# Two transformer blocks in one kernel: a weight slot's lower part moved to GpSimd, a second PSUM bank for one attention head, and an ending with four stores

## What is computed

```python
x = x + _mixer(x, mem, ...);  x = x + _conv_ffn(x, ...)
x = _rmsnorm(x, g1)
h = x
for layer in range(2):
    hn = rmsnorm(h, norm_mix[layer])
    h = h + (hybrid_attention(hn, ...) if layer == 0 else neighbourhood_attention(hn, ...))
    h = h + sq_relu_mlp(rmsnorm(h, norm_ffn[layer]), ffn_w_up[layer], ffn_w_down[layer])
out = rmsnorm(h, final_norm)      # y = x * rsqrt(mean(x*x) + EPS), times the gain
```

## Time and profile before

| | |
|---|---|
| median of 3 runs | 1160.37 us (1159.82 to 1163.45) |
| the profiled execution | 1160.56 us |
| its span, first to last instruction | 1158.7 us |
| TensorE busy | 1143.1 us, 99% |
| VectorE busy | 840.1 us, 73% |
| ScalarE busy | 628.8 us, 54% |
| GpSimd busy | 496.7 us, 43% |
| mean granted TensorE clock | 0.999 of full |

### The profile page before, as it was taken

The page is one execution under the profiler, slowest core; times in us unless marked ns, Lnnn a source line. Parts: engine busy times, 40 slices in busy tenths (PEclk is TensorE's granted clock), DMA queues, the critical chain, the costliest instruction groups (busy, mean ns, idle before and its releaser), DMA issues.

```text
span 1158.7 us, 18483 instructions
## 1 busy us (share of the span) xinstructions
PE 1143.1 (99%) x6964; PEld 1017.0 (88%) x6964; DVE 840.1 (73%) x1099; ACT 628.8 (54%) x858; POOL 496.7 (43%) x433
## 2 busy tenths in 40 slices
PE   8999999999999999999999999999999999999997
PEld 8999999889998888888897888888888888888886
DVE  5778988986675898777898767566576676656655
ACT  7554443556634665555668755444464677444443
POOL 2799997996201543233233538880010455000000
PEclk9999999999999999999999999999999999999999
DMA  9655545563447456554552286655555514565550
GB/s 300 205 179 179 192 161 192 179 203 109 143 156 238 145 182 217 181 186 169 158 161 91 79 236 229 195 191 194 181 182 182 182 38 133 198 200 190 188 181 37
DMA packets 142665, 201.08 MB, mean 174 GB/s; under 512 B 3284, under 2 KB 123092, under 8 KB 142604
## 3 DMA queue, kind: packets, MB, share of 16 engines
q1 hardware_dynamic: 141632, 196.88, 51.5%
q0 software_dynamic: 912, 3.17, 1.2%
q10 hardware_dynamic: 60, 0.20, 0.1%
HBM read 199.20 MB, written 1.05 MB: 173 GB/s over the span
## 4 chain that ended last, share of the span: by engine, by line
PE 95%; DVE 2%; ACT 1%; issue 1%; DMA 0%; POOL 0%; POOLq 0%; DVEq 0%; ACTq 0%
PE ps L2003 52%; PE ps L2046 24%; PE ps L2049 11%; PE ps L2130 3%; PE ps L2045 2%; PE ps L2192 1%; PE ps L2112 1%; PE ps L2180 1%; DMA gates<-in_vecs 0%; ACT ps L758 0%; DVE work L1302 0%; PE ps L2098 0%; PE ps L2396 0%; PE ps L2383 0%; DVE p_parts L1309 0%
## 5 line engine op out<-in xcount | busy, mean ns | idle before, releaser
L1207 DVE TENSOR_TENSOR wlo<-raw,whi 128x2048 fp32r<-128x2048 f32 (+1 forms) x162 | 376.3, 2324 | 132.7 <-ACT whi L668 132.3
L668 ACT ACTIVATE whi<-raw 128x2048 fp32r<-128x2048 f32 (+1 forms) x178 | 337.6, 1897 | 141.0 <-PE ps L2003 133.5
L2046 PE MATMUL ps<-p_parts,whi 128*128 128x512 f32 x1184 | 414.0, 398 | 0.0
L2049 PE MATMUL ps<-p_parts,wlo 128*128 128x256 f32 x1036 | 291.2, 281 | 0.0
L2046 PEld LDWEIGHTS ps<-p_parts,whi 128*128 128x128 f32 x1184 | 216.0, 188 | 41.9
L2049 PEld LDWEIGHTS ps<-p_parts,wlo 128*128 128x128 f32 x1036 | 196.1, 189 | 5.8
L2003 PE MATMUL ps<-p_parts,whi 128*128 128x256 f32 x912 | 164.8, 284 | 0.9 <-DVE p_parts L1234 0.9
L2003 PE MATMUL ps<-whi,q_hi 128*128 128x512 f32 x380 | 148.5, 391 | 0.0
L2003 PE MATMUL ps<-wlo,q_hi 128*128 128x512 f32 x380 | 148.0, 390 | 0.0
L2003 PE MATMUL ps<-whi,q_lo 128*128 128x512 f32 x380 | 148.0, 389 | 0.0
L2003 PEld LDWEIGHTS ps<-p_parts,whi 128*128 128x128 f32 x912 | 142.4, 192 | 1.2 <-issue 1.1
(11 more groups left out here) (322 smaller groups left out, 1907.8 us busy)
## 6 DMA issues: line engine op xcount, KB each, us to landing
raw<-in_w_in SPq DMA_DIRECT2D x35, 1024.0 KB, 5.0
raw<-in_w_up SPq DMA_DIRECT2D x22, 1024.0 KB, 5.1
raw<-in_up_a SPq DMA_DIRECT2D x16, 1024.0 KB, 5.4
raw<-in_down_a SPq DMA_DIRECT2D x16, 1024.0 KB, 4.9
raw<-in_up_b SPq DMA_DIRECT2D x16, 1024.0 KB, 5.5
raw<-in_down_b SPq DMA_DIRECT2D x16, 1024.0 KB, 4.9
raw<-in_od_w_qkv SPq DMA_DIRECT2D x12, 1024.0 KB, 5.1
raw<-in_w_down SPq DMA_DIRECT2D x11, 1024.0 KB, 4.9
```

Source lines behind the costliest of these rows:

```text
L668: nc.scalar.activation(whi[:, g % R, 0:n], raw[:, g % R, 0:n], ACT.Copy).then_inc(hi_ready, 1)
L1207: nc.vector.tensor_tensor(wlo[:, g % R, 0:n], raw[:, g % R, 0:n], whi[:, g % R, 0:n].bitcast(F32), ALU.subtract).then_inc(lo_ready[g % R], 1)
L2046: ins = nc.tensor.matmul(dst, whi[:, r, at], p_parts[:, :, S * k:S * k + S], start=k == 0, stop=k == KD - 1)
L2049: nc.tensor.matmul(dst[:, 0:S], wlo[:, r, at], p_hi[:, S * k:S * k + S], start=False, stop=False)
```

## The change

Three edits. In "att2" the lower part of group G_EVO is no longer one VectorE instruction in `woven_heads`, but four pieces on GpSimd at the start of its own `woven_heads`. In "att3" head 1 gets a bank of its own, bank 4. At the end, VectorE makes the mean square of row tile 0 before its third sum and no longer after it, scales a half of row tile 0 itself (`scaled_half`), and does the last two gain products later; ScalarE scales 512 in place of 1024 columns of row tile 0, ahead of the third square; the stores are four halves in place of a tile and two halves.

```diff
-    ("qk", {0: 4, 2: 4}), ("v", HIGH4), ("att3", HEADS16), ("od_out", HIGH4),
+    ("qk", {0: 4, 2: 4}), ("v", HIGH4), ("att3", {**HEADS16, 2: 15, 4: 1}), ("od_out", HIGH4),
...
 def rows_bank(name, i):
-    if name == "att2" and i == 1:
-        return 5, USES["att2"][5]
-    return 2, USES[name][2] + i - (1 if name == "att2" and i > 1 else 0)
+    second = {"att2": 5, "att3": 4}[name]
+    if i == 1:
+        return second, USES[name][second]
+    return 2, USES[name][2] + i - (1 if i > 1 else 0)
...
-            for done, n, t, part in ((fin_act, 1, 0, slice(0, D)), (fin_dve, 1, 1, slice(0, BW)), (fin_act, 2, 1, slice(BW, D))):
+            for done, n, t, part in ((fin_act, 1, 0, slice(0, BW)), (fin_dve, 1, 0, slice(BW, D)), (fin_dve, 2, 1, slice(0, BW)), (fin_act, 2, 1, slice(BW, D))):
                 sp.wait_ge(done, n)
                 sp.dma_start(out_v[:, t, part], x[:, t, part]).then_inc(out_done, 16)
-            sp.wait_ge(out_done, 16 * 3)
+            sp.wait_ge(out_done, 16 * 4)
...
                 if name == "att2":
+                    for n in range(4):
+                        lo_piece(G_EVO, n)
                     queries_keys(2)
...
             for t, m in FINAL_ORDER:
+                if (t, m) == FINAL_ORDER[2]:
+                    act.wait_ge(fin_y, 1)
+                    scaled_rows(0, slice(0, BW))
                 act.wait_ge(bank_read[4 + t + 2 * m], USES["ffn2b"][4 + t + 2 * m] + 1)
                 square_of_rows("fin2", t, m)
-                if (t, m) == FINAL_ORDER[2]:
-                    act.wait_ge(fin_y, 2)
-                    scaled_rows(0, slice(0, D))
...
                 if name == "att2":
                     maxima(name, 2)
                     maxima(name, 3)
-                    lo(G_EVO)
                     latent_keys_in((4,))
...
+            def scaled_half(t, part):
+                dve.wait_ge(norm_r, T * POW_NORMS.index("fin2") + t + 1)
+                nc.vector.tensor_scalar(x[:, t, part], xfin[:, t, part], rr[:, n + t:n + t + 1], None, ALU.mult).then_inc(fin_dve, 1)
+
             for i, (t, m) in enumerate(FINAL_ORDER):
+                if i == 2:
+                    mean_square(NORMS.index("fin2"), 0)
                 summed(i, t, m)
-                if (t, m) == FINAL_ORDER[2]:
-                    mean_square(NORMS.index("fin2"), 0)
-                times_gain(t, m)
+                if i < 2:
+                    times_gain(t, m)
+            dve.wait_ge(fin_y, 2)
+            scaled_half(0, slice(BW, D))
+            times_gain(*FINAL_ORDER[2])
             mean_square(NORMS.index("fin2"), 1)
-            dve.wait_ge(norm_r, T * POW_NORMS.index("fin2") + 2)
+            times_gain(*FINAL_ORDER[3])
             dve.wait_ge(fin_y, 4)
-            nc.vector.tensor_scalar(x[:, 1, 0:BW], xfin[:, 1, 0:BW], rr[:, n + 1:n + 2], None, ALU.mult).then_inc(fin_dve, 1)
+            scaled_half(1, slice(0, BW))
```

## The result

| | median | spread | ratio to before |
|---|---|---|---|
| before | 1160.37 us | 1159.72 to 1163.45, 10 runs | |
| with the change | 1165.38 us | 1164.51 to 1168.17, 10 runs | 1.0042, 95% 1.0033 to 1.005 |

A forecast was written before the change was run, and what follows sets the result against it. TensorE bounds the kernel, except at the second attention's start, where the chain runs 9 us through VectorE. Terms 3.3 - 0.4 - 0.3 = +2.6 us gave a median of 1163.0 us, range 1159.3 to 1165.2.

The forecast's parts named there:

- Part A: Second attention's start: slot G_EVO's lower part moves from VectorE to GpSimd; +3.3 us, between -0.3 and +4.0.
- the stall: Second attention's first query rotation: VectorE's root and three rotation operations wait for GpSimd pieces, 3.6 us, all on the path.
- The taps of the feed-forward: VectorE operations beside GpSimd pieces from 394.29 us; 4.77 us against 1.66 alone, so 1.04 us more per held operation.
- The 4.3 us: Upper bound of the delay at the first query rotation, if each held operation waits for a whole piece.
- VectorE keeps its turn: Rival at the rotations: 0.45 us wait, then 0.85 at the second rotation; 1160.7 us; chance 0.23 together with no exclusion.
- the move is all gain: Rival: latent key fills readable as early as VectorE is free, 2.9 us gained, 1157.5 us; chance 0.04.
- what the removal gives: Second attention: removing VectorE's 2.19 us instruction brings only 0.28 us through, since VectorE waits for fill 4.
- B: Last attention: head 1 in bank 4 lets head 2's transposes start 0.71 us earlier; -0.4 us in all.
- C: Kernel's end: mean square 0.7 us earlier, but last power 0.93 us in place of 0.55; -0.3 us in all.
- full clock behind the stall: After TensorE's 3.8 us idle before the unit 1 scores, the clock stays full; forecast 1162 to 1164, chance 0.58.
- The range: Whole kernel's time: 1159.3 to 1165.2 us, leaving about 0.06 below and 0.09 above.
- the clock case: Rival: TensorE's 3.8 us idle before the unit 1 scores lowers its clock, 1 to 4 us more, 1164 to 1167; chance 0.15.

The follow-up runs named there:

- the pieces put later: Whole change, but GpSimd starts its four pieces only when VectorE has done both query rotations: 1159.8 us, ratio 0.9996.
- part A alone: Kernel before with only the slot's lower part moved from VectorE to four GpSimd pieces, attention banks and ending as before: 1165.52 us, ratio 1.0047.
- the run with the filled wait: Whole change plus 16 matmuls of no use on TensorE before the scores of unit 1: 1163.11 us, ratio 1.0028.
- one piece: Whole change with one GpSimd instruction of 2048 columns in place of the four pieces: 1165.37 us, ratio 1.0042.

## Why the prediction was wrong

*Part A, the stall: right.* 3.6 us foreseen, 3.63 found in the changed kernel. Its working holds in its parts too: the root held 0.5 us (0.45 foreseen), the first rotation operation free, the next three held for a piece each, 1.29 to 1.40 us from start to start. The taps of the feed-forward were the right rows to price them by. The Trainium skill (SBUF — State Buffer, Who interferes with whom) has the mechanism: the two engines exclude each other for a whole instruction. The trace agrees. The 4.3 us that I had worked out from it took a whole piece of waiting for each held operation (by its own terms it is 0.45 + 3 x 1.25 = 4.2) and is too much, because an operation that gets ready while a piece runs waits only for its rest. The rival that VectorE keeps its turn is refuted by the three held operations, and that the move is all gain is refuted by the 1.76 us wait for fill 4 with nothing held.

*Part A, what the removal gives: right.* 0.28 foreseen, 0.35 found with the pieces put later.

*Parts B and C: right by the traces.* B 0.4 foreseen and 0.37 found, C 0.3 and 0.31, with the last power at 0.93 as foreseen. No run resolves them as times.

*The failed step is the choice of full clock behind the stall: the sum has no term for it.* I had the 3.8 us of idle TensorE (3.66 found), had worked out the price ("1 to 4 us more: 1164 to 1167") and the sign, and then gave it 0.15 with two reasons: "some 4 us passed at the end before the fall, and here work surrounds the gap". Both were wrong. In the changed kernel the clock was full for about 2 us after TensorE stopped (618.26 to near 620.2), where at the end of the kernel before it had been full for some 4. So one fall at one place was no lower bound for another. And the work around the gap didn't shield it: with part A alone the clock fell even after the scores had run. The stretch at half clock cost 2.0 us in the changed kernel, 5.38 - 3.63 + 0.28, and 1.6 and 2.7 in the two other traces with a fall; all lie in the 1 to 4 us of the estimate. It ran the scores in 1.65 us for 0.98 and the four fills in 3.65 for 1.92, and VectorE waited behind them: from the start of the scores to the copy of fill 4 it is 6.15 us, and 4.03 in the run with the filled wait. The run with a filled wait, 1163.11 us, comes to the forecast of 1163.0; the changed kernel is that plus the clock. By the trace that makes 3.35 - 0.7 + 2.0 = 4.7 us, and the medians say 5.0.

*The range* then cut the clock case in half: 1165.2, where that case alone reached to 1167. With only one fall at one place to go by, neither reason against it was strong enough for that cut, nor for a chance of 0.15. The Trainium skill (TensorE: Matmul & The Clock Gate, HAM oscillation) says that waits between groups of matmuls can bring the clock down again and again; I set it aside because the trace of before had no such fall in its middle, but that trace also had no idle time of that length there: behind the kernel's first microseconds its longest wait of TensorE was 0.9 us. The new stall made the condition, and the trace of after agrees with the page in kind: one wait of 3.66 us between matmuls, one fall.

## What to carry to other kernels

Before a subtraction goes to an idle GpSimd, look at what VectorE does in the same microseconds: here each of its operations with two inputs in SBUF that met a running GpSimd subtraction, even one on two columns, waited for its end, and if such operations feed TensorE the free engine is no free place. A wait on one semaphore put the pieces 5 us later and took the whole loss back. When a change makes TensorE wait for several microseconds, price the clock behind it as a term of the sum and not as a remote rival; filling the wait with matmuls of no use shows in one run what the clock's share is.

## What the runs showed that I had not expected

**The delay before the clock falls isn't fixed.** TensorE stopped at 618.26 in the changed kernel and the clock fell near 620.2, 2 us later. With part A alone it stopped at 615.69 and the clock was full until about 621, 5 us later and behind 1.4 us of work. With one piece it stopped at 614.75, and the window 618 to 620 stood at 0.53, which is 0.1 us at full, so it fell near 618.1, 3.4 us later. Idle times of 3.66 to 3.82 us were followed by a fall in all three, one of 2.10 us by none. So the moment at which TensorE stopped doesn't by itself set the moment of the fall, and the work in between didn't keep it off. What a fall costs isn't one number either: 2.0, 1.6 and 2.7 us in these three traces.

**An operation on two columns can wait 4 us.** The root of 128x2 numbers took 0.15, 0.65 or 3.97 us, by how much was left of the GpSimd instruction that it met.

**The engines alternate, and GpSimd pays little.** But for the root and the first rotation operation, which went in together, no two VectorE operations of the first rotation passed at one boundary between two pieces of 512 columns. GpSimd's four pieces took 5.36 us, against 4.98 with no VectorE operation to meet: 0.4 us lost there for 3.6 on VectorE.
